# A streaming encoder layer in float32: norms and wide sums by token tile, and sums over a head's channels from high and low parts

## The reference

```python
xn = rmsnorm(x, g_mix)
p_a, p_b, p_g = split(xn @ w_in)            # RWKV-7 | latent attention | gates
kk = (k * k_k) per head;  kk *= rsqrt(max(sum(kk * kk), 1e-12))
S, y = scan over tokens of the head's state  # 16 heads of 64 channels
mu = mean(y);  var = mean((y - mu) ** 2)     # over a head's 64 channels
y = (y - mu) * rsqrt(var + GN_EPS) * lnx_g + lnx_b + bonus
h = x + (sigmoid(ga) * (y * g) @ w_o_a + sigmoid(gb) * attention @ w_o_b) @ w_out
hn = rmsnorm(h, g_ffn);  gate, up = split(hn @ w_ffn_in)
h = h + (silu(conv3(gate)) * up) @ w_ffn_down
out = rmsnorm(h, g_final)                    # and the new caches and states
```

## Time and profile before

| | us |
|---|---|
| median of three runs (2497.25 to 2504.71) | 2498.18 |
| the profiled execution | 2497.85 |
| its span | 2496.2 |
| PE busy | 2431.5 (97%) |
| DVE busy | 1104.6 (44%) |
| ACT busy | 870.8 (35%) |

### The profile page before, as it was taken

How to read it: one execution, slowest core, us unless ns; L and a number is a source line. 1 busy time by engine, 2 the same in 40 slices (tenths; PEclk the granted TensorE clock), 3 DMA queues, 4 the chain that set the end, 5 groups by cost and what they waited for, 6 DMA issues and landing times.

```text
span 2496.2 us, 44147 instructions
## 1 busy us (share of the span) xinstructions
PE 2431.5 (97%) x17372; PEld 2232.2 (89%) x17372; DVE 1104.6 (44%) x1743; ACT 870.8 (35%) x1311; POOL 108.6 (4%) x182
## 2 busy tenths in 40 slices
PE   6999999999899999999998999999999999999997
PEld 6888888888899999999877999999878999999886
DVE  4555656654433322344333544444233444444234
ACT  4444344443323322344223433333222333333232
POOL 4000000000010100000000000000000000000010
PEclk9999999999999999999999999999999999999999
DMA  5323222222533433344533344444333444444433
GB/s 167 105 74 81 78 77 74 74 72 71 132 119 94 124 98 92 96 127 125 169 124 109 112 126 126 126 126 124 127 126 118 132 126 126 126 127 141 128 129 127
DMA packets 414538, 284.14 MB, mean 114 GB/s; under 512 B 31728, under 2 KB 392690, under 8 KB 413536
## 3 DMA queue, kind: packets, MB, share of 16 engines
q1 hardware_dynamic: 405600, 259.16, 35.3%
q0 software_dynamic: 8832, 23.36, 3.4%
HBM read 275.55 MB, written 6.92 MB: 113 GB/s over the span
## 4 chain that ended last, share of the span: by engine, by line
PE 95%; DVE 2%; ACT 1%; DMA 1%; issue 1%; POOL 0%; DVEq 0%; SPq 0%; POOLq 0%; ACTq 0%
PE banks L1453 20%; PE banks L903 19%; PE banks L907 18%; PE banks L904 18%; PE banks L324 2%; PE banks L916 2%; PE banks L918 2%; PE banks L917 2%; PE banks L392 1%; PE banks L1316 1%; PE banks L472 1%; PE banks L1319 1%; PE banks L457 1%; PE banks L1414 1%; PE banks L485 0%
## 5 line engine op out<-in xcount | busy, mean ns | idle before, releaser
L893 DVE TENSOR_TENSOR w_lo<-w_raw,w_hi 128x1024 fp32r<-128x1024 f32 x482 | 590.1, 1225 | 964.5 <-ACT w_hi L888 964.2
L903 PE MATMUL banks<-x_hi,w_hi 128*128 128x384 f32 x2640 | 918.6, 348 | 8.3 <-DVE w_lo L893 8.3
L907 PE MATMUL banks<-x_hi,w_lo 128*128 128x384 f32 x2640 | 886.9, 336 | 0.0
L904 PE MATMUL banks<-x_lo,w_hi 128*128 128x384 f32 x2640 | 885.7, 335 | 0.0
L888 ACT ACTIVATE w_hi<-w_raw 128x1024 fp32r<-128x1024 f32 x482 | 511.3, 1061 | 1039.9 <-PE banks L907 595.5
L903 PEld LDWEIGHTS banks<-x_hi,w_hi 128*128 128x128 f32 x2640 | 497.6, 188 | 35.6 <-issue 11.9
L904 PEld LDWEIGHTS banks<-x_lo,w_hi 128*128 128x128 f32 x2640 | 498.5, 189 | 5.0 <-issue 0.3
L907 PEld LDWEIGHTS banks<-x_hi,w_lo 128*128 128x128 f32 x2640 | 497.6, 188 | 1.2 <-issue 1.2
L1453 PE MATMUL banks<-w_hi,act_hi 128*128 128x512 f32 x528 | 164.2, 392 | 4.6 <-DVE h_rows L2009 2.4
L1453 PE MATMUL banks<-w_lo,act_hi 128*128 128x512 f32 x528 | 164.2, 392 | 0.0
L1453 PE MATMUL banks<-w_hi,act_lo 128*128 128x512 f32 x528 | 163.2, 390 | 0.0
(11 more groups left out here) (401 smaller groups left out, 2294.4 us busy)
## 6 DMA issues: line engine op xcount, KB each, us to landing
w_raw<-in_w_ffn_in SPq DMA_DIRECT2D x176, 512.0 KB, 4.0
w_raw<-in_w_in SPq DMA_DIRECT2D x144, 512.0 KB, 3.8
w_raw<-in_w_ffn_down SPq DMA_DIRECT2D x88, 512.0 KB, 3.6
w_raw<-in_w_out SPq DMA_DIRECT2D x32, 512.0 KB, 3.6
w_raw<-in_w_o_a SPq DMA_DIRECT2D x16, 512.0 KB, 4.0
w_raw<-in_w_o_b SPq DMA_DIRECT2D x16, 512.0 KB, 3.9
w_raw<-in_w_in SPq DMA_DIRECT2D x20, 256.0 KB, 3.8
w_ukv_head<-in_w_ukv POOLq DMA_DIRECT2D x8, 512.0 KB, 3.9
```

What stands on the lines that cost most here:

```text
L893: nc.vector.tensor_tensor(lo[:, s], raw[:, s], hi[:, s].bitcast(F32), ALU.subtract).then_inc(lo_done, 1)
L903: nc.tensor.matmul(out, hi[:, s, k, :], xh[:, kt, :], start=kt == 0, stop=False)
L904: nc.tensor.matmul(out, hi[:, s, k, :], xl[:, kt, :], start=False, stop=False)
L907: last = nc.tensor.matmul(out, lo[:, s, k, :], xh[:, kt, :], start=False, stop=kt == 15)
```

## The change

1. The three head sums take high and low parts in float32r and two matmuls each (head_sums), with bones_r, a float32r copy of BON. ACT copies the high part, DVE subtracts the low part. The parts lie in regions that are free then (m_t, c_k, c_b).
2. The pieces around the sums move: 2 instead of 1 ahead of the mean, 3 instead of 2 ahead of the variance, and 2 instead of 4 at the turn's end. The transpose of the prompt's state and its copy (state_rows) move behind the variance; the next turn's s_load transposes, no more the lora matmuls, wait for s_out and s0_in.
3. pe_norm turns the first six channel tiles token tile by token tile, as each is scaled. The second block's w_hi and w_lo are made inside the norm, after 8 (first norm) or 12 (second) channel tiles.
4. The first gate tile of the FFN is taken out of the loop and run between the second norm's transposes.
5. In `wide` the last k tile tells DVE when each token tile is done (acc_tile), and add_acc starts with that tile.

```diff
+        def head_sums(out, split):
+            nc.tensor.matmul(out, bon_r[:, :], split[:, 0, :], start=True, stop=False)
+            return nc.tensor.matmul(out, bon_r[:, :], split[:, 1, :], start=False, stop=True)
...
-            pieces(1)
+            pieces(2)
             pe.wait_ge(E("state_done"), f * 4 + 4)
             pe.wait_ge(E("y_raw_done"), f + 1)
-            mm_(ps[:, 3, 0:NT], BON, yb, start=True, stop=True).then_inc(E("mean_ps"), 1)
-            transpose(ps[0:64, 2, 0:P], st[:, :]).then_inc(E("sp_t_ps"), 1)
-            pieces(2)
+            head_sums(ps[:, 3, 0:NT], y_s).then_inc(E("mean_ps"), 1)
+            pieces(3)
             pe.wait_ge(E("sd_done"), f + 1)
             pe.wait_ge(E("y_sq_done"), f + 1)
-            mm_(ps[:, 4, 0:NT], BON, sq_y, start=True, stop=True).then_inc(E("var_ps"), 1)
+            head_sums(ps[:, 4, 0:NT], var_s).then_inc(E("var_ps"), 1)
             if more:
                 pe_kk_sum(f + 1)
             pieces(2)
+            transpose(ps[0:64, 2, 0:P], st[:, :])
             for b in range(NB):
                 last = transpose(ps[0:64, 6 + b // 4, (b % 4) * P:(b % 4 + 1) * P], s0t[:, b, :])
             last.then_inc(E("sd_t_ps"), 1)
             if more:
-                pe.wait_ge(E("s_out"), f + 1)
-                pe.wait_ge(E("s0_in"), f * 32 + 64)
                 pe_lora_g(f + 1)
             pieces(3)
             if more:
+                pe.wait_ge(E("s_out"), f + 1)
+                pe.wait_ge(E("s0_in"), f * 32 + 64)
                 pe_s0(f + 1)
-            pieces(4)
+            pieces(2)
...
-            fn(yb, ps[:, 5, 0:NT], ACT.Copy).then_inc(E("y_raw_done"), 1)
+            fn(yb, ps[:, 5, 0:NT], ACT.Copy)
+            fn(y_s[:, 0, :], ps[:, 5, 0:NT], ACT.Copy).then_inc(E("split_hi"), 1)
             act.wait_ge(E("y_centred"), f + 1)
-            fn(sq_y, yc, ACT.Square).then_inc(E("y_sq_done"), 1)
+            ch.link(fn(sq_y, yc, ACT.Square))
+            fn(var_s[:, 0, :], sq_y, ACT.Copy).then_inc(E("split_hi"), 1)
             cut(5)
...
             act.wait_ge(E("sd_t_ps"), f + 1)
+            act.wait_ge(E("states_stored"), OPEN + f)
+            fn(sto[:, :], ps[0:64, 2, 0:P], ACT.Copy).then_inc(E("s_out"), 1)
             fn(so[:, :, :].rearrange("v (h b) c -> v h (b c)", h=2), ps[0:64, 6:8, :], ACT.Copy)\
...
+            dve.wait_ge(E("split_hi"), f * 3 + 2 + more)
+            tt(y_s[:, 1, :], yb, y_s[:, 0, :].bitcast(F32), S).then_inc(E("y_raw_done"), 1)
+            if more:
+                dve_kk_low(f + 1)
             dve.wait_ge(E("mean_ps"), f + 1)
             stt3(yc, ps[:, 3, 0:NT], -1.0 / 64, yb, M, A).then_inc(E("y_centred"), 1)
             if more:
                 dve_k_mod(ch)
+            dve.wait_ge(E("split_hi"), f * 3 + 3 + more)
+            tt(var_s[:, 1, :], sq_y, var_s[:, 0, :].bitcast(F32), S).then_inc(E("y_sq_done"), 1)
             cut(5)
...
+            for t in range(3):
+                nc.tensor.wait_ge(ready, t + 1)
+                for kt in range(6):
+                    last = turn(t, kt)
+                    if t == 2:
+                        last.then_inc(E("norm_ps"), 1)
...
+            further(range(6, 9))
+            first_gate(range(0, 3))
+            further(range(9, 12))
+            first_gate(range(3, 6))
+            further(range(12, KD))
+            first_gate(range(6, KD))
...
                 for t in range(3):
+                    if t < 2:
+                        dve.wait_ge(E("acc_tile"), done * 2 + (t + 1))
+                    else:
+                        dve.wait_ge(blk_used, need)
```

More of the change, by code:

```diff
@@ L206, in build @@
         n_t, t_x, t_y, t_g = [region(n, [P, 6, 64]) for n in ("n_t", "t_x", "t_y", "t_g")]
-        t_f, m_t, c_k, c_b = [region(n, [P, 6, P]) for n in ("t_full", "m_t", "c_k", "c_b")]
+        t_f = region("t_full", [P, 6, P])
+        kk_off = top[0]
+        m_t = region("m_t", [P, 6, P])
+        y_off = top[0]
+        c_k = region("c_k", [P, 6, P])
+        var_off = top[0]
+        c_b = region("c_b", [P, 6, P])
+        kk_s = at("square_split", [P, 2, NT], kk_off, F32R)
+        y_s = at("y_split", [P, 2, NT], y_off, F32R)
+        var_s = at("y_square_split", [P, 2, NT], var_off, F32R)
         tok = region("tok_major", [P, 3, 3, P])
@@ L220, in build @@
         sto = region("state_rows", [64, P])
+        bon_r = region("bones_r", [P, P], F32R)
         assert top[0] <= 229368, top[0]
@@ L380, in pe_lora_g @@
                 nc.tensor.matmul(ps[:, 5, 0:NT], wg[:, k, :], za[:, 2 + k, :], start=k == 0, stop=k == 1)
+        def head_sums(out, split):
+            nc.tensor.matmul(out, bon_r[:, :], split[:, 0, :], start=True, stop=False)
+            return nc.tensor.matmul(out, bon_r[:, :], split[:, 1, :], start=False, stop=True)
         def pe_kk_sum(f):
             nc.tensor.wait_ge(E("kk_sq_done"), f + 1)
-            nc.tensor.matmul(ps[:, 3, 0:NT], BON, sq[:, :], start=True, stop=True).then_inc(E("kk_sum_ps"), 1)
+            head_sums(ps[:, 3, 0:NT], kk_s).then_inc(E("kk_sum_ps"), 1)
         def pe_s0(f):
@@ L600, in act_gate_sigmoids, with act_kk_square @@
             fn(aa[:, :], ps[:, 3, 0:NT], ACT.Sigmoid, bias=pf[:, 4:5]).then_inc(E("sig_done"), 1)
-        def act_kk_square(f):
+        def act_kk_square(f, ch):
             nc.scalar.wait_ge(E("kk_raw_done"), f + 1)
-            nc.scalar.activation(sq[:, :], kk0[:, :], ACT.Square).then_inc(E("kk_sq_done"), 1)
+            ch.link(nc.scalar.activation(sq[:, :], kk0[:, :], ACT.Square))
+            nc.scalar.activation(kk_s[:, 0, :], sq[:, :], ACT.Copy).then_inc(E("split_hi"), 1)
         def act_exps_early(f):
@@ L668, in act_rwkv @@
             if more:
-                act_kk_square(f + 1)
+                act_kk_square(f + 1, ch)
             cut(4)
@@ L739, in dve_k_mod, with dve_kk_low @@
             ch.link(nc.vector.scalar_tensor_tensor(k2[:, :], t1[:, :], 1.0, z[:, 1, :], ALU.add, ALU.mult))
+        def dve_kk_low(f, first=False):
+            nc.vector.wait_ge(E("split_hi"), 1 if first else f * 3 - 1)
+            nc.vector.tensor_tensor(kk_s[:, 1, :], sq[:, :], kk_s[:, 0, :].bitcast(F32), ALU.subtract)\
+                .then_inc(E("kk_sq_done"), 1)
         def dve_clamp(f):
@@ L939, in dve_next, with pe_norm, further @@
                 dve_lo(t + 1, 0)
[L942 to L951, removed]
+        def pe_norm(src, first, ready):
+            turn = lambda t, kt: transpose(ps[:, 2 + kt % 6, t * P:t * P + P], src[:, t, kt * P:kt * P + P])
+            for t in range(3):
[4 more added lines that the diff above has]
+                        last.then_inc(E("norm_ps"), 1)
+            def further(kts):
+                for kt in kts:
+                    nc.tensor.wait_ge(E("xt_lo"), first * KD + kt - 5)
+                    for t in range(3):
+                        last = turn(t, kt)
+                    last.then_inc(E("norm_ps"), 1)
+            return further
         def act_norm_stats(src, sq_out, arrived, ch):
@@ L964, in build, with act_norm @@
         epsb, gneps = EPS, GN_EPS
-        def act_norm(first, gcol):
+        def act_norm(first, gcol, second, at):
             for kt in range(KD):
+                if kt == at:
+                    act_hi(second, 1)
                 nc.scalar.wait_ge(E("norm_ps"), first * KD + kt + 1)
@@ L970, in act_norm, with dve_norm @@
                                      scale=prm[:, gcol + kt:gcol + kt + 1]).then_inc(E("xh_done"), 1)
-        def dve_norm(first, gcol):
+        def dve_norm(first, gcol, second, at):
             for kt in range(KD):
+                if kt == at:
+                    dve_lo(second, 1)
                 nc.vector.wait_ge(E("xh_done"), first * KD + kt + 1)
@@ L1209, in _ @@
             pe.wait_ge(E("params_done"), 1)
-            pe_norm(xt, 0, E("x_scaled"), E("xt_lo"))
+            pe_norm(xt, 0, E("x_scaled"))(range(6, KD))
             for s in range(2):
@@ L1454, in wide @@
                                            start=kt == 0 and n == 0, stop=kt == kts - 1 and n == 2)
+                        if kt == kts - 1 and t < 2:
+                            last.then_inc(E("acc_tile"), 1)
                     last.then_inc(blk_used, 1)
@@ L1460, in _, with first_gate @@
             pe.wait_ge(E("acc_taken"), OPEN + 2)
-            pe_norm(hn, 1, E("h_scaled"), E("xt_lo"))
-            pe.wait_ge(E("xt_lo"), KD + 8)
+            further = pe_norm(hn, 1, E("h_scaled"))
+            def first_gate(kts):
+                for kt in kts:
+                    pe.wait_ge(E("xt_lo"), KD + kt + 1)
+                    pe_block(T_FFN, kt // 8, ps[:, 0, 0:NT], [kt % 8])
+            further(range(6, 9))
[4 more added lines that the diff above has]
+            first_gate(range(6, KD))
+            for s in range(2):
+                pe_block(T_FFN + 1, s, ps[:, 1, 0:NT])
             for hf in range(2):
-                with pe.Fori(0, HJ) as j:
+                with pe.Fori(1 - hf, HJ) as j:
```

(20 more changed lines are left out.)

10 lines of the change are left out of this document (2 added, 8 removed).

## The result

The changed kernel takes 2531.8 us (median of four executions, 2516.77 to 2536.04) against 2500.39 us for the kernel before, measured beside it: a ratio of 1.0114 with a 95% interval of 1.0069 to 1.0159. It is slower by 31 us. The forecast was 2511 us with a range of 2494 to 2518: the direction was right, the size too small. The profiled execution took 2531.34 us, with a span of 2529.6 us.

A forecast was written before the change was run, and what follows sets the result against it. The prediction took TensorE, busy for 97% of the span, as the bound. The loop's +25.7 us and -12.75 us from norms and wide sums gave +12.95 us on 2497.85 us: 2511 us, range 2494 to 2518.

The forecast's parts named there:

- the third rival: RWKV loop: two waits a turn lower PE's clock, costing 1.5 us a turn more, 2523 us; chance 0.06.
- Waits of pieces 24 and 28: RWKV loop: PE waits for w_lo of two newly opened weight blocks, +2.0 and +2.2 us a turn.
- Head sums: RWKV loop: two split matmuls replace each slower sum, saving 0.30 us three times, -0.9 us a turn.
- Seven turns without the clock: First seven loop turns at +3.3 us each from head sums and both waits, no clock fall: +23.1 us.
- Last turn: Loop's last turn: path runs through w_lo, a weight DMA and ACT's c_square, starting later: +2.9 us.
- First key sum: The key sum ahead of the loop gets the faster split matmuls: -0.3 us.
- first norm: First norm: second block's w_lo goes ahead of eight x_lo; 2.2 us wait goes, last x_lo later: -1.1 us.
- Second norm: Second norm: earlier additions and token-tile transposes let it end sooner, -4.5 us, bounds -2.4 and -5.
- h_rows: Between two wide sums, DVE starts before the third tile ends; three PE waits go: -3.9 us.
- Second half of the FFN and the end: FFN's second half loses a 0.79 us wait, -0.8; only two final additions follow PE's last matmul, -2.45 us.
- the cover holds: Rival for the loop: neither piece 24 nor piece 28 waits, so faster at 2478 us; chance 0.11.
- one of the two waits: Rival for the loop: piece 24 waits but piece 28 does not, 2495 us, no change; chance 0.13.

The follow-up runs named there:

- The run with the new counts alone: The kernel before with only the pieces dealt out as in the changed one (2, 3, 2, 3, 2), head sums still single matmuls: 2537.16 us, ratio 1.0175.
- the runs with one wait at a time: The changed kernel with the weight split issued early for only one block: that of piece 24, 2500.51 us; that of piece 28, 2496.19 us.
- the run with both splits early: The changed kernel with w_hi and w_lo of the blocks opened by pieces 24 and 28 issued earlier: 2474.57 us, ratio 0.9885.

## Why the prediction was off

The step that failed is the pricing of the third rival, "the clock falls too": it was kept out of the sum and given 0.06, because "with the 2.2 us wait near 30 us it stays at 1.00". That was one wait in one execution. The run with the head sums alone has the same wait at the same place, and there the clock fell. Its first matmul, then the stretch behind it:

```profile
31.27 0.44 PE L930 MATMUL banks<-x_hi,w_hi 128*128 128x384 f32 x1 [2.21 <-DVE w_lo L920]
```

```profile
32.00:34.00 2.00, 2.00 (x8) 2.00 (x7) 0.35 (x1) 0.00 (x0) 0.00 (x0) 0.50 0.96 218
```

The run with the new counts alone has it too, 2.21 us up to 31.09, and there the clock holds at 1.00 from 31 to 36. So the row was one draw, not a bound between 2.2 and 3.0 us; and its stretch ends 0.67 us behind the wait, too soon to show what follows (that trace holds 1.00 there as well). The price of 1.5 us for a fall was right (1.54), but one fall a turn was too few: twelve in eight turns, 18.5 us. The upper end of 2518 us left out even the rival's own 2523.

Without the falls the changed kernel's span would have grown by 33.4 - 18.5 = 14.9 us, for the forecast's 12.95. Its four executions point the same way: the one of 2516.77 us had a mean granted clock of 0.988, within the 0.986 to 0.991 of the kernel before, and the three of 2531.34 to 2536.04 us had 0.981 to 0.982.

The other terms, by what they measured:

- *Waits of pieces 24 and 28*, +2.0 and +2.2: 2.20 and 2.29, by the runs with one wait at a time. The chains behind them were right, w_lo to 0.02 us at piece 24. Of the causes that the prediction names, the moved pieces weigh most; its lower bound of 1.4 us without the new copy came out as 1.29.
- *Head sums*, -0.9 a turn: -0.88, by the run with both splits early.
- *Seven turns without the clock*: 7 x (2.20 + 2.29 - 0.88) = +25.3 for the forecast's +23.1. *Last turn*: 5.75 less two falls is +2.7 for +2.9. With the falls: 25.3 + 2.7 + 18.5 = 46.5, and the loop measured 46.6 against 25.7.
- *First key sum*, -0.3, *and first norm*, -1.1: -0.4 together, and the run without the head sums starts its loop at 105.21 against 105.18, so the norm gave nothing. The 2.2 us wait did go. But the transposes by token tile complete the first k tile only with their thirteenth transpose, where it was the third:

```profile
20.29 4.29 DVE L1012 SCALAR_TENSOR_TENSOR x_lo<-banks,params,x_hi 128x384 fp32r<-128x384 f32 x8 [1.31 <-ACT x_hi L1004]
24.54 1.23 DVE L920 TENSOR_TENSOR w_lo<-w_raw,w_hi 128x1024 fp32r<-128x1024 f32 x1
25.68 4.29 DVE L1012 SCALAR_TENSOR_TENSOR x_lo<-banks,params,x_hi 128x384 fp32r<-128x384 f32 x8
```

  VectorE's x_lo start at 20.29 in place of 19.02, and the w_lo in their middle adds 1.1. The last ends at 29.97, not at 27.5, and PE stands 0.78 and 1.16 us for x_lo among the transposes. The prediction counted the second delay, not the first.
- *Second norm*, -4.5: the wait fell by 4.6 and the stretch behind it grew by 0.3, so -4.3. *h_rows*, -3.9: gone. *Second half of the FFN and the end*, -0.8 and -2.45: the stretch with the former shrank by 2.8, of which 1.45 is h_rows; the latter is -2.5. All stretches outside the loop together gave -13.1 for the forecast's -13.05 (with the first key sum). So close a fit is in part luck: the first norm fell short and the FFN gave more, this compares one execution of each kernel, and the run with these hunks alone gave 10.9 us by its median.

That "the cover holds" and "one of the two waits" had small chances was right: both waits came in every turn.

## What to carry to other kernels

Work that is moved forward to cover a chain has inputs of its own: here every fourth piece opens a block whose split stood in line behind that very chain, so the cover caused a wait of 2 us where the bare chain made a turn 0.4 us longer than before. Look first whether the operand that comes late can be issued in a gap of its engine, as both splits could here. A new idle stretch of TensorE is priced as its length plus a chance of the clock's fall behind it, taken from many such waits and not from a single one; in these runs a wait of 2 us cost 2.2 to 2.3 us, and 1.54 us more where a fall followed.

## What the runs showed that was not expected

- The same 2.2 us wait near 31 us left the clock at 1.00 in two profiled executions and was followed by 0.50 in a third. Single waits a turn, of 1.97 to 2.87 us, were followed by a fall in nine of sixteen cases; with two a turn it was twelve of sixteen in the changed kernel and eleven in the one with the head sums alone.
- Eleven useless matmuls in fifteen of the sixteen waits, 2.07 us each time, made the changed kernel faster by 21.6 us; the sixteenth, left empty, was followed by a fall.
- PE loses some 0.2 us more at a wait than its idle time: waits of 1.97 and 2.02 us cost 2.20 and 2.29 us in a turn's length.
